# Loading the first tokens in pieces between the weight pieces, with angles and selection rounds placed elsewhere, in a two-layer encoder kernel

## What is computed

```python
h = _rms_norm(x, norm_mix)
z = jnp.einsum('bsd,de->bse', h, w_in)
za, bq, bk, bv, cq, clat, ciq, cik, ciw, zd, zg = _split(z, IN_SIZES)
ya = _gmlp_mixer(jax.nn.gelu(za), ...)       # A: products over a chunk of 128 tokens
yb = _swa_sink_mixer(...)                    # B: sliding-window attention, 8 heads, rotated q and k
yc = _dsa_mixer(...)                         # C: attention over the 64 keys that an index score selects
yd = _pool_mixer(zd, d_w_group, d_scale)     # D: means over the last 2, 4, 8, 16 tokens
gates = jax.nn.sigmoid(zg).reshape(Bsz, S, N_BRANCH, D_MODEL)
merged = sum over the branches of gates[:, :, i] * (y_i @ w_out_i)
x = x + merged @ w_o
h2 = _rms_norm(x, norm_ffn)
gate, up = jnp.split(h2 @ w_gate_up, 2, axis=-1)
return x + (jax.nn.silu(gate) * up) @ w_down
```

## Time and profile before

| | us |
|---|---|
| median of 3 runs | 824.48 |
| lowest and highest of them | 820.76, 826.37 |
| the profiled execution | 821.93 |
| its span, from first to last instruction | 820.2 |
| TensorE busy | 805.8 (98%) |
| VectorE busy | 558.1 (68%) |
| ScalarE busy | 405.6 (49%) |
| GpSimd busy | 56.2 (7%) |

### The profile page before, as it was taken

One profiled execution on the slowest core, in us unless ns is written; L12 is line 12 of the kernel. 1 busy time (PEld: TensorE's weight loads), 2 busy tenths in 40 slices (PEclk: granted clock), 3 DMA queues, 4 the chain that ended last, 5 costly groups with the idle time before them and its releaser, 6 DMA issues.

```text
span 820.2 us, 10243 instructions
## 1 busy us (share of the span) xinstructions
PE 805.8 (98%) x3868; PEld 658.6 (80%) x3868; DVE 558.1 (68%) x844; ACT 405.6 (49%) x558; POOL 56.2 (7%) x103
## 2 busy tenths in 40 slices
PE   8899899999999999999999998999999999999998
PEld 7688677777888888888888886777788888888886
DVE  7689789875675654466568887898675764565443
ACT  6756456553364434444366644654542644444430
POOL 8450000000000000000005100000000000000000
PEclk9999999999999999999999999999999999999999
DMA  9644446546375564665663625375545565665541
GB/s 302 209 144 145 152 154 205 171 138 205 110 250 177 184 203 154 204 204 178 172 225 122 231 78 181 122 217 181 174 154 190 172 203 156 207 202 185 175 154 51
DMA packets 98672, 144.38 MB, mean 176 GB/s; under 512 B 11064, under 2 KB 62016, under 8 KB 98624
## 3 DMA queue, kind: packets, MB, share of 16 engines
q1 hardware_dynamic: 98624, 143.73, 54.0%
HBM read 142.54 MB, written 1.05 MB: 175 GB/s over the span
## 4 chain that ended last, share of the span: by engine, by line
PE 87%; DVE 5%; POOL 3%; issue 2%; DMA 1%; ACT 1%; DVEq 0%; POOLq 0%; ACTq 0%; SPq 0%
PE big L1500 18%; PE big L1504 17%; PE big L1503 17%; PE mix L1504 10%; PE mix L1500 10%; PE mix L1503 10%; DVE w_lo L1029 1%; DMA w_raw<-in_w_in 1%; PE mix L1865 1%; PE mix L1544 1%; PE mix L1633 1%; PE mix L1568 1%; PE mix L1588 1%; PE mix L1621 0%; POOL logits L683 0%
## 5 line engine op out<-in xcount | busy, mean ns | idle before, releaser
L729 ACT ACTIVATE w_hi<-w_raw 128x2048 fp32r<-128x2048 f32 (+3 forms) x142 | 257.0, 1814 | 158.6 <-DMA w_raw<-in_w_gate_up 88.0
L1029 DVE TENSOR_TENSOR w_lo<-w_raw,w_hi 128x2048 fp32r<-128x2048 f32 (+3 forms) x142 | 304.6, 2161 | 30.5 <-ACT w_hi L729 29.3
L1500 PE MATMUL big<-w_hi,act_hi 128*128 128x512 f32 (+2 forms) x476 | 186.2, 391 | 3.0 <-DVE w_lo L1029 3.0
L1503 PE MATMUL big<-w_lo,act_hi 128*128 128x512 f32 (+2 forms) x476 | 181.7, 382 | 0.0
L1504 PE MATMUL big<-w_hi,act_lo 128*128 128x512 f32 (+2 forms) x476 | 181.6, 381 | 0.0
L1500 PE MATMUL mix<-w_hi,act_hi 128*128 128x512 f32 x352 | 137.4, 390 | 0.0
L1504 PE MATMUL mix<-w_hi,act_lo 128*128 128x512 f32 x352 | 137.1, 390 | 0.0
L1503 PE MATMUL mix<-w_lo,act_hi 128*128 128x512 f32 x352 | 137.0, 389 | 0.0
L1500 PEld LDWEIGHTS big<-w_hi,act_hi 128*128 128x128 f32 x476 | 89.5, 188 | 24.4 <-issue 6.2
L1504 PEld LDWEIGHTS big<-w_hi,act_lo 128*128 128x128 f32 x476 | 89.4, 188 | 17.3
L1288 DVE TENSOR_TENSOR y_h_lo<-mix,y_h_hi 128x256 fp32r<-128x256 f32 x44 | 16.6, 420 | 126.9 <-ACT y_h_hi L948 126.9
(11 more groups left out here) (207 smaller groups left out, 714.1 us busy)
## 6 DMA issues: line engine op xcount, KB each, us to landing
w_raw<-in_w_in SPq DMA_DIRECT2D x44, 1024.0 KB, 5.1
w_raw<-in_w_gate_up SPq DMA_DIRECT2D x88, 512.0 KB, 4.8
w_raw<-in_w_down SPq DMA_DIRECT2D x22, 1024.0 KB, 4.9
w_raw<-in_w_o SPq DMA_DIRECT2D x8, 1024.0 KB, 5.1
w_raw<-in_b_w_out SPq DMA_DIRECT2D x4, 1024.0 KB, 6.1
w_raw<-in_w_in SPq DMA_DIRECT2D x3, 904.0 KB, 5.0
w_raw<-in_w_in SPq DMA_DIRECT2D x4, 512.0 KB, 3.9
w_raw<-in_a_w_out SPq DMA_DIRECT2D x4, 512.0 KB, 3.5
```

Source lines behind the costliest of these rows:

```text
L729: nc.scalar.activation(high(u)[:, a:b], arrived(u)[:, a:b], ACT.Copy).then_inc(hi_ready, 1)
L1029: nc.vector.tensor_tensor(low(u)[:, a:b], arrived(u)[:, a:b], high(u)[:, a:b].bitcast(F32), ALU.subtract).then_inc(lo_ready, 1)
L1500: ins = nc.tensor.matmul(dst[:, 0:w], xh, wh, start=first and n == 0, stop=False)
L1503: nc.tensor.matmul(dst[:, 0:w], xh, wl, start=False, stop=False)
```

## The change

Four things are changed. The tokens are loaded in pieces of 512 columns (half of the channels of a block), which stand between the pieces of unit 0; the gains and the positions are issued by ScalarE. TensorE makes four products of zeros at the start and four more after its first four transposes; each half is turned, gained and rounded on its own, the first half of both blocks before the second. GpSimd makes the angles first and the averages after the first power. The selection rounds of slot 12 stand in slot 13, in both layers.

```diff
-TOPK_AT = {12: (0, 0, 3), 15: (0, 3, 4), 16: (0, 4, 6), 17: (0, 6, 8), 18: (1, 0, 2), 20: (1, 2, 4), 21: (1, 4, 5),
+TOPK_AT = {13: (0, 0, 3), 15: (0, 3, 4), 16: (0, 4, 6), 17: (0, 6, 8), 18: (1, 0, 2), 20: (1, 2, 4), 21: (1, 4, 5),
...
 SyncE
-            def load_tokens(tb):
-                sp.dma_start(xs[:, tb], x[0, tok(tb)]).then_inc(x_in[tb], 16)
+            def load_tokens(tb, h):
+                cols = slice(h * N, (h + 1) * N)
+                sp.dma_start(xs[:, tb, cols], x[0, tok(tb), cols]).then_inc(x_in[tb][h], 16)
...
                         if half == 0:
-                            load_tokens(1)
-                            load_positions()
+                            load_tokens(1, 0)
+                    for tb in range(TB):
+                        load_tokens(tb, 1)
...
-            load_tokens(0)
-            load_gain(0)
+            load_tokens(0, 0)
...
 GpSimd (the averages' code is moved unchanged into averages_of_pools)
+            pool.wait_ge(const_pool, POOL_ANGLES)
             pool.wait_ge(pos_in, 16)
...
                 for name in NORMS:
                     power(l, name)
+                    if (l, name) == (0, "mix"):
+                        averages_of_pools()
...
 ScalarE
+            def load_rows():
+                act.dma_start(gain_rows, norm_mix[0].rearrange("(k p) -> k p", p=P)).then_inc(gain_in.sem, 16)
+                act.dma_start(pos_i[:], positions[0].rearrange("(t p) -> p t", p=P),
+                              allow_slow_non_contiguous=True).then_inc(pos_in, 16)
...
                 if l == 0:
+                    load_rows()
                     split(0, 0, 0)
-                    high_gained(0, "hT", 0)
+                    high_gained(0, "hT", 0, [0])
+                    high_gained(0, "hT", 1, [0])
                     split(0, 0, 1)
-                    high_gained(0, "hT", 1, [0])
-                    x_squares(0, "mix", 0)
+                    high_gained(0, "hT", 0, [1])
+                    high_gained(0, "hT", 1, [1])
                     split(0, 1, 0)
                     split(0, 1, 1)
-                    high_gained(0, "hT", 1, [1])
-                    x_squares(0, "mix", 1)
+                    for tb in range(TB):
+                        x_squares(0, "mix", tb)
...
 VectorE
                     gain_half(0, "hT", 0, 0)
-                    gain_half(0, "hT", 0, 1)
                     split(0, 0, 0)
                     gain_low(0, "hT", 0, 0)
                     gain_half(0, "hT", 1, 0)
                     split(0, 0, 1)
                     gain_low(0, "hT", 1, 0)
-                    gain_low(0, "hT", 0, 1)
-                    gain_half(0, "hT", 1, 1)
+                    for tb in range(TB):
+                        gain_half(0, "hT", tb, 1)
+                        gain_low(0, "hT", tb, 1)
                     split(0, 1, 0)
-                    gain_low(0, "hT", 1, 1)
                     split(0, 1, 1)
...
 TensorE
-            for _ in range(3):
-                nc.tensor.matmul(big[:, 3, 0:SEQ], zeros[:, 0:P], zeros[:, 0:SEQ], start=True, stop=True)
+            products_of_zeros(4)
...
-                    turn(l, "hT", 0)
+                    turn(l, "hT", 0, [0])
+                    products_of_zeros(4)
                     first_products(0, 0)
-                    turn(l, "hT", 1)
-                    for half, kind in ((0, 1), (0, 2), (1, 0), (1, 1), (1, 2)):
-                        first_products(half, kind)
+                    turn(l, "hT", 1, [0])
+                    for kind in (1, 2):
+                        first_products(0, kind)
+                    turn(l, "hT", 0, [1])
+                    for kind in range(3):
+                        first_products(1, kind)
+                    turn(l, "hT", 1, [1])
```

More of the change, by code:

```diff
@@ L320, in trunk_kernel @@
         params_in = signal("params_in", 16 * N_PARAMS)
-        x_in = [sem(f"x_in{tb}") for tb in range(TB)]
+        x_in = [[sem(f"x_in{tb}{h}") for h in range(2)] for tb in range(TB)]
         pos_in = sem("pos_in")
@@ L706, in power, with averages_of_pools @@
                                         ).then_inc(rstd_ready.sem, 1)
+            def averages_of_pools():
+                done = POOL_ANGLES
+                pool.wait_ge(averages, N_AVERAGES)
+                for tile, width in ((pool_a, SEQ), (pool_b, P)):
+                    nc.gpsimd.affine_select(out=tile[:], in_=tile[:], compare_op=ALU.is_ge, fill=0.0, base=0,
+                                            pattern=[[0, len(D_POOLS)], [1, width]], channel_multiplier=-1
+                                            ).then_inc(const_pool, 1)
+                done += 2
+                pool.wait_ge(const_pool, done)
+                for g, w in enumerate(D_POOLS):
+                    for tile, width in ((pool_a, SEQ), (pool_b, P)):
+                        nc.gpsimd.affine_select(out=tile[:, g, :], in_=tile[:, g, :], compare_op=ALU.is_ge,
+                                                fill=0.0, base=w - 1, pattern=[[-1, width]], channel_multiplier=1
+                                                ).then_inc(const_pool, 1)
+                done += 2 * len(D_POOLS)
+                pool.wait_ge(const_pool, done)
+                for g, w in enumerate(D_POOLS):
+                    for tile, first in ((pool_a, w - 1), (pool_b, 0)):
+                        at = tile[:, g, first:P]
+                        nc.gpsimd.affine_select(out=at, in_=at, compare_op=ALU.not_equal,
+                                                fill=float(np.float32(1.0 / w) - np.float32(1.0)), base=-first,
+                                                pattern=[[-1, P - first]], channel_multiplier=1
+                                                ).then_inc(const_pool, 1)
+                done += 2 * len(D_POOLS)
+                assert done == POOL_CONSTS
             for l in range(DEPTH):
@@ L740, in x_squares @@
                 else:
-                    act.wait_ge(x_in[tb], 16)
+                    for h in range(2):
+                        act.wait_ge(x_in[tb][h], 16)
                     for c in range(2):
@@ L1526, in first_products, with turn @@
                                      start=kind == 0 and k == 0, stop=False)
-            def turn(l, stage, tb):
-                if stage == "hT":
-                    pe.wait_ge(x_in[tb], 16)
+            def turn(l, stage, tb, halves=range(2)):
                 src = merged if stage == "mT" else xs
-                for h in range(2):
+                for h in halves:
                     bank = mix_bank(stage, tb, h)
+                    if stage == "hT":
+                        pe.wait_ge(x_in[tb][h], 16)
                     if stage == "mT":
@@ L1745, in _, with products_of_zeros @@
             zeros = rope_t[:].rearrange("p h d -> p (h d)")
-            for _ in range(3):
-                nc.tensor.matmul(big[:, 3, 0:SEQ], zeros[:, 0:P], zeros[:, 0:SEQ], start=True, stop=True)
+            def products_of_zeros(n):
+                for _ in range(n):
+                    nc.tensor.matmul(big[:, 3, 0:SEQ], zeros[:, 0:P], zeros[:, 0:SEQ], start=True, stop=True)
+            products_of_zeros(4)
             pe.wait_ge(const_pool, POOL_IDENT)
```

9 lines of the change are left out of this document (2 added, 7 removed).

## The result

The changed kernel takes 817.93 us, the median of 7 runs from 817.42 to 818.34; the kernel before, on the same chip beside it, 823.12 (820.76 to 826.37). The ratio is 0.9934, with an interval of 0.9911 to 0.9957: 0.66% faster, clear of no change but within the 1% that counts as the same. 821.0 was forecast, in a range of 815.5 to 826.0. The profiled execution is 818.05 us with a span of 816.3, against 821.93 and 820.2: the span fell by 3.9 us where the sum said 3.4. The median fell by more, 5.2, and that difference is the larger lesson.

The account below looks back on a forecast made before the run. TensorE, busy 805.8 of 820.2 us, was taken to bound the kernel. The rounds' -4.9 and the start's +1.5 sum to -3.4 us: 818.5 profiled, median 821.0, range 815.5 to 826.0.

Parts of the forecast that it names:

- the sum: Whole kernel: -4.9 for the selection rounds and +1.5 for the start make -3.4 us, a profiled execution of 818.5.
- The rounds: Index scores, both layers: moving the selection rounds removes TensorE's waits for exponentials, -2.4 and -2.5, together -4.9 us.
- the cover ahead of `y_d_lo`: VectorE's idle 3.91 us ahead of `y_d_lo` hides the moved rounds' 3.2 us, with 0.7 us to spare.
- The start: Start through `bq`: serial hand-over between VectorE and ScalarE delays `kv`; `bq`'s second half starts at 39.2, +1.5 us.
- The angles: GpSimd to ScalarE's sine: the 4.89 us wait goes, but ScalarE comes to the angles 0.5 us later than before.
- The clock: TensorE at the start: full clock after new waits of 2.2 and 1.2 us; a drop would cost 0.5 us.
- rival 4: Waits before 19 and 25 us leave TensorE at half clock through `kv`: +7.7 us, 832.2; chance 0.05.
- Rival 2: The start gains as well, ScalarE not losing 5.4 us and the angles' wait won: -7.9, 816.6; chance 0.2.
- 3: The wait at the scores stays or moves to the probabilities' transposes; rounds bring 1 in all: 825.0; chance 0.15.
- the last one, from the profiled execution to the median: Whole kernel: profiled 821.93 lies 2.55 under the median 824.48, so profiled 818.5 would mean a median of 821.0.

Follow-up runs that it names:

- the start alone: The changed kernel with the selection rounds back in slot 12, keeping its loads, zeros, start order and angles' place: 825.19 us, ratio 1.0013 to the kernel before.
- the rounds alone: The kernel before with one edit, the selection rounds of slot 12 moved to slot 13 in both layers: 815.74 us, ratio 0.9906.
- the order woven: The changed kernel with splits and squares put back between the gains, roundings and low parts on ScalarE and VectorE: 814.38 us, ratio 0.9890 to the kernel before.

## Why the prediction was right, and where it was off

**The rounds, -4.9 forecast.** Right in size and in mechanism. Both waits for exponentials (5.0 us) are gone, `y_ac_lo` starts at `y_ac_hi`'s end (89.83 against 89.86), and the cover ahead of `y_d_lo` held in both layers: 0.7 us to spare was forecast, 1.21 was left. The rounds took 3.05 in their new place, 3.2 was allowed. By the distance from the product ahead of the scores to the scores, the two waits were worth 5.1: a wait in the profile is counted from the end that it models for that product, and the next one would have started before that.

**The start, +1.5 forecast.** Right, step by step, against the profiled execution of before:

| step | forecast | measured |
|---|---|---|
| first product | 8.2 | 8.59 |
| wait for unit 1, its end | 2.2, 19.0 | 2.21, 19.43 |
| ScalarE done with unit 3 | 24.8 | 24.7 |
| `kv` starts after a wait of | 25.3, 1.2 | 25.42, 0.80 |
| the sine, with no wait | 26.1 | 26.00 |
| `bq` first, second half | 36.4, 39.2 | 36.42, 39.14 |

That is +1.5 at `bq` (39.14 against 37.65) and +1.35 at the product ahead of the scores (93.32 against 91.97). The sum is then 5.1 less 1.35, about 3.75, and 3.9 was measured. Where the 0.15 in each place went was not looked for.

**The angles, their 4.89 us as no gain of their own.** Right: that their wait would go because ScalarE is late itself was shown by putting them back, at no change.

**The clock.** Full clock was assumed behind the new waits, and the profiled execution had it (1.00 from 16 to 24 us, below). The price of a drop there was put at 0.5 us; without the second zeros, and in the run with the start alone, it happened, and cost nothing. But rival 4, a clock that stays low through `kv`, has only this much to it: the drops seen end within about 3.5 us.

```profile
16.00:20.00 4.00, 1.79 (x9) 1.00 0.99 302
20.00:24.00 4.00, 4.00 (x21) 1.00 0.44 116
```

**Rival 2 is refuted, and 3 didn't happen.** The start is no gain; by the ratios it costs 2.3 us with the rounds moved (0.9934 against 0.9906), more than 1.5, in line with an old start that did 1.2 better in the profiled execution of the rounds alone than in that of before. With the rounds in slot 12 it costs 1.1 (1.0013), with an interval from nothing to 2.3; why the two differ was not settled.

**The step that failed is the last one, from the profiled execution to the median.** The prediction took the 2.55 us by which the profiled execution of before lay under the median as an offset that stays, and got 821.0. The changed kernel's median is 0.12 under its own profiled execution. Two things were in that offset. Some of it was a median of three runs: seven gave 823.12, and the larger batches 823.75 and 823.78, which leaves 1.2 to 1.9. The rest, and most of the scatter of 5.6 us, was the price of drops in TensorE's clock behind the very waits that the rounds take away. That term, about 2.8 us of the median, was missing from the sum, which allowed for a drop only at the start; it is the main reason why the median came out at 817.93, 3.1 below the forecast, with a span that was 0.5 below it. It would have been further below, had the start not cost 2.2 or 2.3 at the median instead of 1.5: that these two errors have opposite signs was luck.

## What to carry to other kernels

Where two engines hand a buffer back and forth, put other work between the two halves of each hand-over: with the same loads and the same instructions, the order alone was worth 3.7 us here. Before an offset between one profile and the median is carried over, compare the granted clock and the span over all executions: if the longer executions have the lower clocks, the waits of TensorE may cost more than the profile shows, and removing them gives that back too. Filling the wait with products is the test. And price each edit against what is late next: early angles were worth about 1 us with one start and nothing with the other. The earlier load of unit 5 brought 0.9 with the order woven; with the changed kernel's order it was not tried.

## What the hardware showed that was not expected

**An idle TensorE pays twice, but not always.** After idle times of 2.2 to 2.5 us the granted clock fell to 0.50 for about 3 us in some executions and not in others (at the start of layer 0 also after 1.73 us). Each drop at the scores cost some 1.5 us, and the two were worth about 2.8 us of the median. The executions of the kernel before spanned 818.9 us at a mean granted clock of 1.0, and 824.6 at 0.989; between these ends the two do not go strictly together (822.1 at 0.998, 819.4 at 0.996). Kernels whose waits at the scores were taken away or filled varied by 0.3 to 1.7 us. What decides in one execution was not settled.

**GpSimd is slowed by VectorE.** While VectorE subtracts weights in two long instructions (22.91 to 27.91 us in the changed kernel), one instruction of GpSimd takes 2.34 us instead of the 0.40 of the same shape behind it, as its timeline shows:

```profile
25.84 2.34 POOL L687 TENSOR_SCALAR_AFFINE_SELECT pool_a<-pool_a 128x256 f32<-128x256 f32 x1
...
28.39 0.40 POOL L687 TENSOR_SCALAR_AFFINE_SELECT pool_a<-pool_a 128x256 f32<-128x256 f32 x1
```

The Trainium skill (SBUF — State Buffer, SBUF: two separate sides) says that an instruction of VectorE with two inputs in SBUF and one of GpSimd that reads it exclude each other for their whole length; the trace agrees, the long one ends at 28.2, just behind VectorE's. So the end of a chain on GpSimd seems to depend on when VectorE does its splits. The angles of the old start ended at 25.6 us in one execution and 24.45 in another. In the changed kernel with the averages first they began at the same 11.5 us as in the latter and ended at 21.6, and there VectorE's two long subtractions began only at 22.2 instead of 19.1. No run here kept VectorE still to measure the chain alone.

**A record and a pace that disagree.** With the rounds alone, TensorE's first products, from 9.6 to 13 us, stood 0.45 us apart, and products of the same shape 0.21 from 15 us on, while the granted clock of that stretch reads 1.00. In the same way the changed kernel's first four products of zeros took 0.93 us each and its second four 0.49, at a granted clock that reads 1.00 for both. Why the two disagree was not settled; the distance of the starts is the safer reading there, and the mean clock of an execution misses what a slow stretch like this one costs.
